# Eight sample rows' queries, keys and gate values by column quarters, with a later summing product, in a one-core hybrid decoder layer

## The reference

```python
h = rmsnorm(x, ln1_g)
z = einsum('btd,dc->btc', h, w_in)             # 1024 -> 2560 columns
u, va, q, k, v = split(z)                      # 512 columns each
q, k = rope(q, pos), rope(k, pos)
a_out = u * (causal_spatial(w_s) @ rmsnorm(va, g_v) + b_s)
b_out = merge(dilated_attention(q, k, v))      # three (window, dilation) patterns
x = x + concat(a_out, b_out) @ w_out
x = x + hier_moe(rmsnorm(x, ln2_g))            # top-2 of 8 experts in the best of 4 groups
y = rmsnorm(x, lnf_g)
```

## Time and profile before

| what | value |
|---|---|
| median of 3 runs (lowest, highest) | 435.73 (434.81, 436.08) |
| the profiled execution, its own time | 435.69 |
| its span, first to last instruction | 433.7 |
| mean granted clock of PE | 0.974 |
| PE, DVE, ACT, POOL busy | 394.5, 214.3, 150.7, 70.4 |

### The profile page before, as it was taken

How to read it: one execution, slowest core, us unless ns; L and a number is a source line. 1 busy time by engine, 2 the same in 40 slices (tenths; PEclk the granted TensorE clock), 3 DMA queues, 4 the chain that set the end, 5 groups by cost and what they waited for, 6 DMA issues and landing times. The chain is left out here.

```text
span 433.7 us, 6404 instructions
## 1 busy us (share of the span) xinstructions
PE 394.5 (91%) x2466; PEld 210.6 (49%) x2466; DVE 214.3 (49%) x442; ACT 150.7 (35%) x321; POOL 70.4 (16%) x59
## 2 busy tenths in 40 slices
PE   1999999979998999998989998969999999999782
PEld 1444444434443444455534567756555555554650
DVE  2969699695375464374441535831222322222266
ACT  5715211223444564455431436111222322222043
POOL 0002454470100100000000000220323223211000
PEclk9999999989999999999999998879999999999898
DMA  8982764881405233830169994899899999994484
GB/s 290 352 256 68 278 192 158 332 288 55 142 0 196 98 116 107 271 140 1 49 253 410 410 416 126 321 358 387 316 411 410 411 410 406 405 405 173 133 327 193
DMA packets 42323, 109.17 MB, mean 252 GB/s; under 512 B 7864, under 2 KB 8632, under 8 KB 42288
## 3 DMA queue, kind: packets, MB, share of 16 engines
q1 hardware_dynamic: 36000, 94.79, 59.3%
q0 software_dynamic: 5856, 12.81, 7.9%
q10 hardware_dynamic: 432, 1.11, 0.7%
HBM read 100.00 MB, written 16.94 MB: 270 GB/s over the span
## 5 line engine op out<-in xcount | busy, mean ns | idle before, releaser
L1548 PE MATMUL bank<-weights_split,tokens_split 128*128 128x512 f16 (+1 forms) x648 | 149.0, 383 | 1.5 <-DVE x L1267 1.4
L1548 PEld LDWEIGHTS bank<-weights_split,tokens_split 128*128 128x128 f16 (+1 forms) x648 | 61.2, 97 | 79.4 <-issue 10.1
L1859 PE MATMUL bank<-big,tokens_split 128*64 128x256 f32 x320 | 38.4, 394 | 1.5 <-ACT tokens_split L949 1.5
L637 POOL TENSOR_TENSOR big<-big,middle 128x1536 f32<-128x1536 f32 x8 | 27.8, 3477 | 62.7 <-DMA middle<-sample_q 40.1
L1445 DVE TENSOR_TENSOR middle<-bank,middle 128x128 f32<-128x128 f32 x16 | 4.7, 292 | 58.6 <-ACT middle L954 58.6
L1859 PEld LDWEIGHTS bank<-big,tokens_split 128*64 128x64 f32 x320 | 23.6, 142 | 13.4 <-ACT tokens_split L949 2.1
L1808 PE MATMUL bank<-half_consts 128*128 128x256 f16 x186 | 23.8, 294 | 2.4 <-issue 2.4
L671 POOL DMA_INDIRECT tokens_split<-h_rows,middle x16 | 16.2, 1015 | 59.9 <-PE bank L1848 46.8
L1522 PE MATMUL bank<-ident,big 128*128 128x128 f32 (+1 forms) x92 | 14.6, 294 | 12.3 <-DVE big L1033 9.5
L826 ACT ACTIVATE middle<-bank 128x128 f32<-128x128 f32 (+3 forms) x32 | 13.9, 435 | 29.5 <-PE bank L1597 29.3
L1023 DVE SCALAR_TENSOR_TENSOR weights_split<-middle,weights_split 128x1024 f16<-128x1024 f32 x16 | 23.0, 1471 | 0.2
(11 more groups left out here) (199 smaller groups left out, 540.6 us busy)
## 6 DMA issues: line engine op xcount, KB each, us to landing
big<-in_w_gate SPq DMA_DIRECT2D x10, 1024.0 KB, 13.9
big<-in_w_up SPq DMA_DIRECT2D x10, 1024.0 KB, 17.4
big<-in_w_down SPq DMA_DIRECT2D x10, 1024.0 KB, 15.3
middle<-in_w_in SPq DMA_DIRECT2D x16, 512.0 KB, 7.0
big<-in_cache_win_k SPq DMA_DIRECT2D x24, 256.0 KB, 4.6
middle<-in_cache_win_v SPq DMA_DIRECT2D x24, 256.0 KB, 4.6
big<-in_w_out SPq DMA_DIRECT2D x8, 512.0 KB, 7.3
big<-expert_rows SPq DMA_DIRECT2D x8, 512.0 KB, 6.8
```

The source lines that it names most:

```text
L637: nc.gpsimd.tensor_tensor(prod[:, :, :], kring[:, b % 2], qb[:, b % 2, :].unsqueeze(1).to_broadcast([P, NPAT, W]), ALU.mult).then_inc(prod ...
L1548: ins = T.matmul(out, (hT if rows is None else rows)[:, high_low, k if rows is None else k - 4, tokens], wg[:, place, part, k, columns], s ...
L1859: ins = T.matmul((ptb, ovb)[b][e * CAP:(e + 1) * CAP, 0:2 * FE], xT[:, b, k, e * CAP:(e + 1) * CAP], places[slot][:, 0:2, e, k * FE:(k + 1 ...
```

## The change

- The sample rows' q, k and va no longer pass through `project` and a bank of `acc`. `entry_part(kind)` does the 24 products in four groups of 32 output rows (`by_quarters`, shared with `quarters`), ACT copies the bank (`copy_entry_part`), and one tile or so later `entry_sum(kind)` sums the four groups with `fold`. Part and sum use `sbk[0]`, `ovb` and `tp[0]`.
- The copy takes all 128 rows of the bank, so PE first fills `sbk[0]` and `ovb` with eight products of ones.
- PE's order changes: `scores(0)` goes behind va's tile 1 and `scores(1)` behind tile 3; `turn_qk` of the last two k tiles go behind va's tile 0.
- DVE rotates the sample queries before the low half of prompt tile 3, on the sum instead of `acc`. Each of its other steps keeps its place.
- `small` (it holds `fold`) is read by ACT's queue at the start instead of SP's. POOL sends the keys out before its multiply 6 instead of 5.

```diff
-UNITS = [("q", t) for t in ENTRY] + [(_kind, t) for _kind in ("k", "va") for t in TILES]
+UNITS = [(_kind, t) for _kind in ("q", "k", "va") for t in range(NT - 1)]
+ENTRY_PARTS = ["q", "k", "va"]
...
+        entry_partial = cut(big, 20992, 512)
...
-            sp.dma_start(small[:, :], const[:, C_M100:C_END]).then_inc(consts_in, 16)
...
-                if b == 5:
+                if b == 6:
                     pool.wait_ge(k_ready, NT)
...
+            act.dma_start(small[:, :], const[:, C_M100:C_END]).then_inc(small_in, 16)
...
+            def copy_entry_part(kind):
+
+                n = ENTRY_PARTS.index(kind)
+                act.wait_ge(sample_part, n + 1)
+                nc.scalar.activation(entry_partial, (ovb if kind == "va" else sbk[0])[:, :],
+                                     ACT.Copy).then_inc(sample_part_copied, 1)
+
+            copy_entry_part("q")
             turn_h(ENTRY[4])
...
-                turn(("k", t), kT[:, :, cols(t)])
-            turn(("k", NT - 2), kT[:, :, cols(NT - 2)])
+                if t == 1:
+                    copy_entry_part("k")
+                if t < 2:
+                    turn(("k", t), kT[:, :, cols(t)])
...
             for t in range(NT):
+                if t == NT - 2:
+                    copy_entry_part("va")
                 va(t)
+                if t == 0:
+                    turn(("k", 2), kT[:, :, cols(2)])
+                    turn(("k", 3), kT[:, :, cols(3)])
                 if t < PIECES:
                     split_high(3, t)
...
-                dve.wait_ge(acc_ready, u + 1)
+                if whole:
+                    dve.wait_ge(acc_ready, UNIT[(kind, t)] + 1)
+                else:
+                    dve.wait_ge(sample_sum, ENTRY_PARTS.index(kind) + 1)
...
+            rope("q", ENTRY[2])
             low_h(ENTRY[4])
-            rope("q", ENTRY[2])
...
+            def by_quarters(out, group):
+
+                for i, (high_low, part) in enumerate(((0, 0), (0, 1), (1, 0))):
+                    for j in range(2):
+                        for g in range(4):
+                            ins = T.matmul(out[32 * g:32 * g + NS, :], hT[:, high_low, 2 * g + j, SEQ:SEQ + NS],
+                                           wg[:, group % 2, part, 2 * g + j, :],
+                                           start=i == 0 and j == 0, stop=i == 2 and j == 1)
+                return ins
+
+            def entry_part(kind):
+
+                n = ENTRY_PARTS.index(kind)
+                pe.wait_ge(w_split, PIECES * (W_ORDER.index(kind) + 1))
+                if kind == "q":
+                    wait_turned_out(pe, ("h", 2 * NT - 1))
+                if kind == "va":
+                    pe.wait_ge(k_ready, NT)
+                by_quarters(ovb if kind == "va" else sbk[0], n).then_inc(sample_part, 1)
+
+            def entry_sum(kind):
+
+                n = ENTRY_PARTS.index(kind)
+                pe.wait_ge(sample_part_copied, n + 1)
...
+                T.matmul((tp[0] if kind == "va" else ovb)[0:NS, :], fold, entry_partial,
+                         start=True, stop=True).then_inc(sample_sum, 1)
+
+            pe.wait_ge(ones_set, 1)
+            for c in range(4):
+                for bank in (sbk[0], ovb):
+                    T.matmul(bank[:, c * P:(c + 1) * P], ones[:, :], ones[:, :], start=True, stop=True)
```

More of the change, by code:

```diff
@@ L1036, in rope @@
             def rope(kind, t):
[L1038 removed]
                 n = rows_of(t)
+                whole = t < NT - 1
+                bank = acc[UNIT[(kind, t)] % 2] if whole else ovb
                 dst = kn[0:n, t] if kind == "k" else (qn[0:n, t % 2] if t < NT - 1 else qs[0:n])
[L1041 removed]
+                z = bank[0:n, 0:W].rearrange("p (h n) -> p h n", h=HEADS)
                 d3 = dst.rearrange("p (h n) -> p h n", h=HEADS)
@@ L1053, in rope @@
                 V.tensor_tensor(t3[:, :, 0:half], z[:, :, half:HD], tb(sin, 0, half), ALU.mult)
-                V.tensor_tensor(t3[:, :, half:HD], z[:, :, 0:half], tb(sin, half, HD), ALU.mult).then_inc(free_d, 1)
-                dve.wait_ge(free_d, evacuated(u)[1])
+                ins = V.tensor_tensor(t3[:, :, half:HD], z[:, :, 0:half], tb(sin, half, HD), ALU.mult)
+                if whole:
+                    ins.then_inc(free_d, 1)
+                    dve.wait_ge(free_d, evacuated(UNIT[(kind, t)])[1])
+                else:
+                    step(ins)
                 V.tensor_tensor(dst, dst, turned_half, ALU.add).then_inc(q_ready if kind == "q" else k_ready, 1)
@@ L1126, in va @@
             def va(t):
-                n, u = rows_of(t), UNIT[("va", t)]
-                z, inverse_times = [bank[0:n, 0:W] for bank in (acc[u % 2], ptb)]
+                n, whole = rows_of(t), t < NT - 1
+                z = (acc[UNIT[("va", t)] % 2] if whole else tp[0])[0:n, 0:W]
+                inverse_times = ptb[0:n, 0:W]
                 r8, y8 = stat[0:n, 48:56], stat[0:n, 56:64]
@@ L1134, in va @@
                 step(V.reciprocal(y8, r8))
[L1135 to L1139, removed]
+                ins = V.scalar_tensor_tensor(out=inverse_times.rearrange("p (h n) -> p h n", h=HEADS),
+                                             in0=z.rearrange("p (h n) -> p h n", h=HEADS), scalar=UNDO,
+                                             in1=y8.unsqueeze(2).to_broadcast([n, HEADS, HD]),
+                                             op0=ALU.mult, op1=ALU.mult)
+                if whole:
+                    ins.then_inc(free_d, 1)
+                    dve.wait_ge(free_d, evacuated(UNIT[("va", t)])[1])
+                else:
+                    step(ins)
                 V.tensor_tensor(vn[0:n, t], inverse_times, gvb[0:n], ALU.mult).then_inc(va_ready, 1)
@@ L1574, in _ @@
+            turn_h(ENTRY[2])
+            project(("q", 1))
+            turn_h(ENTRY[3])
+            entry_part("q")
+            entry_sum("q")
+            turn_h(ENTRY[4])
+            turn_qk("q", 0)
+            project(("q", 2))
+            turn_qk("q", 1)
+            project(("q", 3))
+            turn_qk("q", 2)
             project(("k", 0))
-            turn_qk("q", NT - 2)
+            turn_qk("q", 3)
             project(("k", 1))
-            for t in range(2, NT):
-                project(("k", t))
-                turn_qk("k", t - 2)
+            project(("k", 2))
@@ L1580, in scores @@
+            turn_qk("k", 0)
+            entry_part("k")
+            project(("k", 3))
+            turn_qk("k", 1)
+            entry_sum("k")
             def scores(c):
@@ L1667, in quarters @@
                 pe.wait_ge(w_split, PIECES * (group + 1))
[L1668 to L1674, removed]
+                by_quarters(acc[u % 2], group).then_inc(acc_ready, 1)
             def quarters_sum(what, unit):
@@ L1705, in turn_head @@
                 turns((kind, t), quarter(uu[:, t]))
[L1707 to L1713, removed]
+            project(("va", 0))
+            turn_qk("k", 2)
+            turn_qk("k", 3)
+            project(("va", 1))
+            scores(0)
+            project(("va", 2))
+            entry_part("va")
+            project(("va", 3))
+            scores(1)
+            entry_sum("va")
             project(("v", 0))
```

40 lines of the change are left out of this document (24 added, 16 removed).

## The result

The changed kernel took 430.25 (median of three runs, 428.02 to 432.2), the kernel before 435.9 in the same rounds. A run of 436.89 counts as slow (over 1.5% above the fastest run of its kernel) and is left out of medians and ratios, as are two runs of the quarters alone further down. The ratio is 0.986, 95% interval [0.9817, 0.9904]: faster, by 5.6 between the medians. Timed again with the experiments, six runs: 430.84 (429.05 to 433.58), which is 4.6 under the kernel before beside it, 0.9894 [0.9843, 0.9945]. The forecast was 429.0, so the sign and the range held, and the gain is 1 to 2 short of the 6.8 forecast. The profiled execution took 430.25.

A forecast was written before the change was run, and what follows sets the result against it. It took the entry as bound by PE, with DVE almost as full; the first task at 103.1 for 111.20 gained 8.1, one clock drop returned 1.3, giving 429.0, with 8 in 10 within 426.8 to 431.8.

The forecast's parts named there:

- the 6.8 forecast: Whole kernel: first softmax task 8.1 earlier, 1.3 returned by one clock drop, so 6.8 gained.
- Part, sum, the two lists: Entry stage: part plus sum cost PE 2.49 for 5.34, three times; PE's and DVE's lists must both be followed.
- The new wait in q: Q stage: PE idles from 31.0 to about 32.85, so the stage gains only 1.2 of 2.85.
- DVE's way from va's tile 0 to the first softmax row: DVE in the entry: 29.57 less waits of 3.64 plus 0.85, from 76.2 to 103.0.
- kept for the range: V's first weight piece lands at 79.7, ACT free at 78.5: nothing or 1.2 lost, left out of the sum.
- rival 4: DVE later still, by v's weights or POOL's multiplies: 2 to 3 us more, 431 to 432; chance 0.06.
- the signs that I had set: Wrong if va's tile 0 passes 71, v's tile 0 waits for weights, q/k clock is 0.5, or an 8-earlier first task's end isn't.
- One clock drop of 1.3, at the first task: PE's 2.3 gap before the first softmax task drops the clock once, costing 1.3; chance 0.42, 429.0.
- The Trainium skill's rule that transposes do not count as work for the clock: Q stage, 28.1 to 33.35: only the sum counts, drop certain, 428.9 or 430.2; two drops had chance 0.17.
- A shift of the first task reaches the end: After the entry: an earlier first softmax task (111.20 before) carries whole through the softmax and expert stages.
- rival 5: Expert stage set by its weights' transfers, so the gain is given back later: 435 or so; chance 0.05.
- The 8.6 saved on PE: Sample rows' q, k and va products on PE: 2.85 less, three times, 8.6.

The follow-up runs named there:

- the quarters alone: The changed kernel with both pairs of score products back in their old places, against the kernel before: 433.25, ratio 0.9935.
- the second profile: Another profile of the unaltered changed kernel, from its repeat timing against the kernel before: median 430.84, ratio 0.9894.
- the rotation turned back: The changed kernel with DVE rotating the sample queries after the low half of prompt tile 3 again: 429.93 once, then 429.05, ratio 0.9864.
- three small edits elsewhere: On the changed kernel: sample-query rotation after the low half, v's weights one step earlier, last sum behind the second softmax scaling: 425.8, ratio 0.9777.
- the three kernels without quarters: Kernel before (435.73); it with only the scores moved (429.54); that with v's weights earlier and the last sum later too (431.73).
- the scores alone: The kernel before with only the two pairs of score products moved behind va's tiles 1 and 3: 429.54, ratio 0.985.

## Why the prediction was right or wrong

- *Part, sum, the two lists.* Right: 2.49 for 5.34. va's tile 0 on PE at 68.98 for 69.4 predicted, on DVE at 75.79 for 76.2.
- *The new wait in q* of about 1.85, because the rotation stands ahead of the low half: right (1.94), and shown by turning them round.
- *The term that was mis-sized* is DVE's way from va's tile 0 to the first softmax row. I took off the 2.23 and 1.41 that DVE waited for PE, put in 0.85 for ACT's turns and nothing for the landing of v's weights, though the median landing alone gave 1.2, which I "kept for the range". It came out as 104.84 - 75.79 = 29.05 for 26.8. The transfer was issued when I said (72.86 for 72.7), but ACT had its first piece after 7.96, not the median 7.0. Before, the same transfer was issued at 74.25:

```profile
74.25 2.50 SPq L475 DMA_DIRECT2D middle<-in_w_in  x4
```

DVE wanted that piece only at 83.33, 9.08 later, and took it without a wait, since it had stood until 80.69 for va's tile 0. In the changed kernel DVE was ready 5.6 after the issue (at 78.50): the cover was gone, and a wait of 3.41 took the place of the two removed. This is rival 4, in a smaller size: 1.8 at the first task. By the signs that I had set, it is also one of being wrong, a wait for weights inside v's tile 0 (2.29); the other is the clock of 0.50 in the q stage of the second profile.

- *One clock drop of 1.3, at the first task.* One there was in most profiles, but in the q stage: 1.68 on PE, 1.06 at the first task (78.36 to 79.42). Of the two profiles of the change itself the first was without it. The Trainium skill's rule that transposes do not count as work for the clock (TensorE: Matmul & The Clock Gate, Part 4: PE-mode transpose) named that place, and by my reading of it the fall was certain. The trace agrees in six profiles of seven; a stretch of the same rows held 1.00 in the seventh. It also held in the three profiles with the rotation turned back, which have the same sum and transposes there and 0.88 less idle time. No run here parts the transposes from the idle time between them.
- *A shift of the first task reaches the end.* Right in the main: from there to the down product of the last expert pair (399.49 before, 392.85 after) it is 288.3 before and 286.0 to 288.8 in the others, with no order by the first task, so rival 5 falls for the change. That scatter of 2.8 between single profiles is as large as several differences told here, and in six of the other kernels PE stands once, for 0.3 to 2.0, for an expert's weights. The last stage gave 1.2 back: 34.2 from that row to the end of the span before, 35.45 after.
- *What the gain came from.* Not asked in the forecast, and the largest surprise: moving 8 score products gains as much alone, and the quarters alone gain 2.5. The 8.6 saved on PE became 1.4 at the first task beyond that (79.75 to 78.36), or 0.3 with the clock's fall, because DVE, v's weights and the q stage's gap were in the way. With those eased, the change gives 9.65.

So the sum of 6.8 less 1.8 for v's weights is 5.0, and 4.6 and 5.6 were measured. That it comes so close is luck in part. In the profiled execution the drop of 1.3 at the first task did not come, and the last stage, for which the sum had no term, gave back 1.2 in its place; in the second profile the clock fell, but in the q stage.

## What to carry to other kernels

Before crediting a saving on a full engine, list what the other engine will wait for when its old waits go: a transfer that was always in time beside a wait may be next in line. Look for a gap that an edit of order opens and price the clock behind it, with more than one profile, since the same gap kept the clock once and lost it the next time. And time each half of a two-part change by itself: here the smaller half alone gained as much as both, and the larger one added to it only after three small edits elsewhere.

## What the runs showed that I had not expected

A transfer of the same 512 KB pieces landed 7.3 to 8.0 after its issue behind the loads of one sequence's keys and query in one queue, and in at most 5.5 ahead of them, while those then landed later. Near the end PE stops in every kernel, behind a flag that it loads and branches on, and in most kernels with quarters a second time after five products that only keep the clock up; timeline of the changed kernel:

```profile
397.60 1.25 PE L1889 MATMUL bank<-half_consts 128*128 128x256 f16 x5 [2.81 <-issue]
401.35 11.82 PE L1889 MATMUL bank<-half_consts 128*128 128x256 f16 x95 [2.50 <-issue]
```

The second stop is missing in the three kernels without quarters and in the one with 24 more products in va's part, where the last stage took 33.49 for 35.45. What the stop costs is not shown by that: with the scores alone, which lack it, the last stage took 36.06, and with the rotation turned back, which has it, 34.4 in one profile. Its cause is open; no run was made for it.
